# A decoder layer's last expert quad: the final weights spread in two parts between transposes and down products, and one way back put ahead of the last product

## What is computed

```python
for g in range(N_GROUPS):
    hid = (silu(einsum('nd,edf->nef', hf, w_gate[g]))
           * einsum('nd,edf->nef', hf, w_up[g]) * combine[:, g, :, None])
    out = out + einsum('nef,efd->nd', hid, w_down[g])
...
x = x + out
return rmsnorm(x, final_norm_g)     # x * rsqrt(mean(x*x) + eps) * g, g of 1024
```

## Time and profile before

| | us |
|---|---|
| median of 3 runs | 439.71 |
| lowest and highest | 438.43, 440.27 |
| the profiled execution, its own time | 438.02 |
| its span, first to last instruction | 436.3 |
| TensorE busy | 395.9 (91%) |
| VectorE, ScalarE busy | 190.4 (44%), 155.0 (36%) |
| mean granted TensorE clock | 0.979 of 2.4 GHz |

### The profile page before, as it was taken

How to read it: one execution, slowest core, us unless ns; L and a number is a source line. 1 busy time by engine, 2 the same in 40 slices (tenths; PEclk the granted TensorE clock), 3 DMA queues, 4 the chain that set the end, 5 groups by cost and what they waited for, 6 DMA issues and landing times.

```text
span 436.3 us, 7016 instructions
## 1 busy us (share of the span) xinstructions
PE 395.9 (91%) x2761; PEld 278.0 (64%) x2761; DVE 190.4 (44%) x358; ACT 155.0 (36%) x299; POOL 36.0 (8%) x80
## 2 busy tenths in 40 slices
PE   7999999999999999999999989899878838758984
PEld 7998897777788888999796634434333303313632
DVE  3675667866667846754655211221212102102123
ACT  6633565576358444485737110100000000001013
POOL 4010122224000000010401200000000000000001
PEclk9999999999999999999999999999999959969999
DMA  7978776767777668897758899999999999999993
GB/s 243 302 223 281 231 263 215 235 206 241 258 241 268 202 232 292 276 332 225 270 218 361 331 424 421 415 420 421 422 422 423 421 421 422 421 421 409 409 380 120
DMA packets 48770, 138.95 MB, mean 318 GB/s; under 512 B 5191, under 2 KB 19559, under 8 KB 39528
## 3 DMA queue, kind: packets, MB, share of 16 engines
q1 hardware_dynamic: 48528, 138.31, 85.0%
q10 hardware_dynamic: 216, 0.28, 0.2%
HBM read 137.54 MB, written 1.05 MB: 318 GB/s over the span
## 4 chain that ended last, share of the span: by engine, by line
PE 75%; DMA 12%; SPq 5%; DVE 3%; ACT 1%; issue 1%; POOL 1%; DVEq 0%; POOLq 0%; ACTq 0%
DMA moe_pair<-in_expert_w_up_dram 12%; PE proj L1407 10%; PE proj L1408 9%; PE proj L1409 9%; PE proj L1833 7%; SPq L428 5%; PE score L1760 4%; PE score L1856 4%; PE attno L1408 2%; PE attno L1409 2%; PE attno L1407 2%; PE attno L1905 2%; PE proj L1787 2%; PE attno L1551 1%; PE probt L1409 1%; PE probt L1408 1%
## 5 line engine op out<-in xcount | busy, mean ns | idle before, releaser
L945 DVE TENSOR_TENSOR w_lo<-w_raw,w_hi 128x1024 fp32r<-128x1024 f32 x64 | 78.3, 1226 | 37.1 <-ACT w_hi L682 36.8
L682 ACT ACTIVATE w_hi<-w_raw 128x1024 fp32r<-128x1024 f32 x64 | 67.9, 1060 | 40.4 <-DMA w_raw<-in_w_in_dram 11.1
L1833 PE MATMUL proj<-moe_pair,moe_x 128*32 128x512 f32 x384 | 47.4, 637 | 19.6 <-DMA moe_pair<-in_expert_w_up_dram 19.6
L1317 DVE TENSOR_TENSOR moe_x<-score,gains_moe 128x256 f32<-128x256 f32 x32 | 13.6, 425 | 93.3 <-PE score L1760 93.1
L887 ACT ACTIVATE hid<-proj 128x256 f32<-128x256 f32 x8 | 3.1, 383 | 136.8 <-PE proj L1833 112.8
L1833 PEld LDWEIGHTS proj<-moe_pair,moe_x 128*32 128x32 f32 x384 | 11.8, 116 | 45.9 <-issue 44.8
L1760 PEld LDWEIGHTS score<-sel,xg 128*128 128x128 f32 x256 | 30.5, 192 | 10.6 <-issue 10.0
L1407 PE MATMUL proj<-hT_hi,w_hi 128*128 128x256 f32 x112 | 32.3, 288 | 0.8 <-DVE w_lo L1024 0.8
L1760 PE MATMUL score<-sel,xg 128*128 128x128 f32 x256 | 32.5, 279 | 0.0
L1409 PE MATMUL proj<-hT_hi,w_lo 128*128 128x256 f32 x112 | 31.7, 283 | 0.0
L1408 PE MATMUL proj<-hT_lo,w_hi 128*128 128x256 f32 x112 | 31.7, 283 | 0.0
(11 more groups left out here) (345 smaller groups left out, 731.9 us busy)
## 6 DMA issues: line engine op xcount, KB each, us to landing
moe_pair<-in_expert_w_gate_dram SPq DMA_DIRECT2D x28, 1024.0 KB, 13.2
moe_pair<-in_expert_w_up_dram SPq DMA_DIRECT2D x28, 1024.0 KB, 15.0
moe_pair<-in_expert_w_down_dram SPq DMA_DIRECT2D x27, 1024.0 KB, 24.9
w_raw<-in_w_in_dram SPq DMA_DIRECT2D x33, 512.0 KB, 4.4
moe_pair<-in_expert_w_down_dram SPq DMA_DIRECT2D x10, 512.0 KB, 6.5
w_raw<-in_xattn_wkv_dram SPq DMA_DIRECT2D x8, 512.0 KB, 4.4
w_raw<-in_mix_out_w_dram SPq DMA_DIRECT2D x8, 512.0 KB, 5.0
moe_pair<-in_expert_w_gate_dram SPq DMA_DIRECT2D x8, 512.0 KB, 20.1
```

The costliest lines, as they stand in the source:

```text
L682: act.activation(w_hi[g % NS][:], w_raw[:, g % NW], ACT.Copy).then_inc(hi_done, 1)
L945: dve.tensor_tensor(w_lo[g % NS][:], w_raw[:, g % NW], w_hi[g % NS][:].bitcast(F32), ALU.subtract)\
L1317: dve.tensor_tensor(moe_x[:, pair], SC[u % 2][:, 0:2 * P].rearrange("p (k s) -> p k s", k=2), gains_moe[:, u // 2, pair].unsqueeze(2) .bro ...
L1833: op = pe.matmul(PJ[0][e * WIN:(e + 1) * WIN, :].rearrange("p (j f) -> p j f", j=2), moe_x[:, k % 4, e * WIN:(e + 1) * WIN], pair[:].rearr ...
```

## The change

The spreads leave `gate_up_by_columns`. The first one (now into `PJ[0]`) stands behind the transposes, before TensorE waits for `hidT`; the second (still into `SC[1]`) stands between the first and the second half of `down_first_columns`. VectorE's two copies to `fin_g` move behind the product that makes `hid` and behind the copy to `selwT`. TensorE's wait for both copies (`fin_g_set`) moves from before the transposes to before the first ways back.

The way back of tile 0 for piece 0 moves ahead of the last product, `down_last_columns(1, 1)`, with its wait for VectorE's copy of that piece. The others follow as: tile 1 piece 0, tile 0 piece 1, tile 1 piece 1. Each now counts its own semaphore step, and ScalarE's wait for the last half is one higher.

```diff
@@ ScalarE
-                    act.wait_ge(back_ps[t][half], more * 2 + 4)
+                    act.wait_ge(back_ps[t][half], more * 2 + 4 + half)
@@ VectorE, behind the copy to selwT
                 if next_experts is None:
+                    for h, bank in enumerate((PJ[0], SC[1])):
+                        dve.wait_ge(fin_g_ps, h + 1)
+                        dve.tensor_copy(fin_g[:, h * 512:(h + 1) * 512], bank[:]).then_inc(fin_g_set, 1)
                     dve.wait_ge(fin_g_set, 2)
@@ TensorE
+            def spread_gains(bank, half):
+
+                pe.matmul(bank[:], ones_row[:], g_row[:, half * 512:(half + 1) * 512], start=True, stop=True)\
+                    .then_inc(fin_g_ps, 1)
...
             def back_last_columns(t, i):
 
+                pe.wait_ge(y1_sb_set, i + 1)
...
+                    .then_inc(back_ps[t][1], 1)
...
                 gate_up_by_columns(LAST_QUAD, n, ends_in, LAST_UP)
+                transposes(n, hid_halves)
+                pe.wait_ge(fin_in, 16)
+                pe.wait_ge(ones_row_set, 1)
+                spread_gains(PJ[0], 0)
+                pe.wait_ge(hidT_sb, n + 1)
+                down_first_columns(0)
+                pe.wait_ge(selT_sb, n + 1)
+                spread_gains(SC[1], 1)
+                down_first_columns(1).then_inc(y0_ps, 1)
                 pe.wait_ge(fin_g_set, 2)
-                transposes(n, hid_halves)
-                pe.wait_ge(hidT_sb, n + 1)
-                down_first_columns().then_inc(y0_ps, 1)
-                pe.wait_ge(selT_sb, n + 1)
                 pe.wait_ge(y_act, n + 1)
...
                 down_last_columns(0, 1).then_inc(y1_ps, 1)
+                back_last_columns(0, 0)
                 pe.wait_ge(last_cols_in, 16)
                 down_last_columns(1, 1).then_inc(y1_ps, 1)
+                back_last_columns(1, 0)
                 for t in range(TT):
-                    for i in range(2):
-                        pe.wait_ge(y1_sb_set, i + 1)
-                        op = back_last_columns(t, i)
-                    op.then_inc(back_ps[t][1], 1)
+                    back_last_columns(t, 1)
```

More of the change, by code:

```diff
@@ L1328, in expert_quad @@
                 dve.wait_ge(slots_moved, n + 1)
[L1329 to L1332, removed]
                 dve.wait_ge(silu_done, n + 1)
@@ L1797, in gate_up_by_columns @@
                     for j in range(2):
[L1798 to L1804, removed]
                         for pair in range(2):
@@ L1877, in down_whole, with down_first_columns @@
                 return op
[L1879 to L1886, removed]
-                return op
+            def down_first_columns(kt):
+                c = GU_CHUNKS + kt
+                pe.wait_ge(ends_in[c], LAST_LANDED)
+                w = slots[slot_of_chunk(LAST_QUAD * MOE_CHUNKS + c)]
+                for e in range(QE):
+                    op = down_product(0, kt, e, w[:, e * 512:(e + 1) * 512])
+                return op
+            def spread_gains(bank, half):
+                pe.matmul(bank[:], ones_row[:], g_row[:, half * 512:(half + 1) * 512], start=True, stop=True)\
+                    .then_inc(fin_g_ps, 1)
             def down_last_columns(i, kt):
@@ L1898, in back_last_columns @@
             def back_last_columns(t, i):
-                return pe.matmul(ACC[t][1][:, i * CW:(i + 1) * CW], selwT[:, t * P:(t + 1) * P],
-                                 y1_last[:, i * CW:(i + 1) * CW], start=False, stop=True, skip_group_check=True)
+                pe.wait_ge(y1_sb_set, i + 1)
+                pe.matmul(ACC[t][1][:, i * CW:(i + 1) * CW], selwT[:, t * P:(t + 1) * P],
+                          y1_last[:, i * CW:(i + 1) * CW], start=False, stop=True, skip_group_check=True)\
+                    .then_inc(back_ps[t][1], 1)
             def back_to_tokens(t, half):
```

## The result

The changed kernel takes 442.96 us (median of 4 runs, 441.23 to 443.06) against 439.89 us for the kernel before (4 runs). The ratio is 1.0078, with a 95% interval of 1.0062 to 1.0094: 3.4 us slower by the ratio and 3.1 us between the medians, where 1.0 us was forecast. The profiled execution took 441.23 us, the shortest of the four, with a span of 439.5. That is 3.2 us more than the span before, so the two traces side by side show a loss of the full size.

What follows compares the result with a forecast made beforehand. TensorE's chain from 416 us, with load landings close behind, was taken as the bound. Terms of −0.19, +1.31 and −0.07 gave +1.05, taken as +1.0 on 439.7: 440.7 us, range 438.9 to 442.0.

Steps and rivals of the forecast that it cites:

- three signs that I had named: Signs of a wrong forecast: last product before 428.2, a load holding it, or a clock row not 1.00 up to 431.
- The bounds: End of the kernel from 416 us: TensorE's chain with load landings close behind; landings stay, up products start at 416.7.
- Part 1: Spreads moved from in front of the up products: −1.91 + 0.38 + 0.34 + 1.00, a gain of 0.19 us.
- the price of a change of shape: First instruction behind a wait or change of shape takes 0.1 longer, so each moved spread was taken as 1.0 us.
- The bound that I named, 0: Lower limit of the gain from moving the spreads: 0 if each spread costs 1.1 us.
- The wait for `fin_g_set`: Wait for VectorE's copies, now before the first ways back: priced at nothing, with 0.9 us in hand.
- Part 2: Way back ahead of the last product: that product 1.31 us behind its place in the queue, VectorE's scaling 1.05 later.
- The wait of 0.73: Before the moved way back, TensorE waits 0.73 us for VectorE's copy of the third small product's result.
- The way back itself: The moved way back, two instructions ahead of the last product: 0.54 us plus 0.04 for the change of shape.
- The clock: TensorE's granted clock over the tail: expected at 1.00 up to 431, adding nothing to the sum.
- the rival that names it: Clock halves in the new pause before 428.7, the work left takes twice as long: +3.3 us, 443.0; chance 0.04.
- the new pause: TensorE's new wait of 0.7 us behind the third small product, taken as short against the earlier 7.8 us.

Runs made afterwards that it cites:

- the two versions with the old tail: Changed kernel with the second spread in the wait for ScalarE's copy and last ways back in old order: 0.9990 with one-row spreads, 0.9986 with 128-row spreads.
- the part alone: Kernel before with only the new order of the last ways back, spreads left in front of the up products: ratio 1.0022.
- full_rows: Changed kernel with both spreads over all 128 rows (127 rows of zeros behind the weights' row), same order and waits: ratio 1.0031, median 440.71 us.
- filled_wait: Changed kernel plus two unused 128-row products in TensorE's wait before the first ways back, spreads still one row: ratio 1.0053.
- part1_only: Changed kernel with the ways back of the last columns in their old order, spreads still one row: ratio 1.0030, median 441.06 us.

## Why the prediction was wrong, step by step

Two of the three signs that I had named did not come: the last product started at 430.83, not before 428.2, and no load held it. The third came, a clock row that is not 1.00 up to 431.

**The bounds: right.** The up products began at 416.76 for 416.7, and the landings stayed. The last landing proved to be the floor, as the two versions with the old tail show.

**Part 1: the sign was wrong by a small size.** The transposes (419.25 for 419.20) came as worked out. The term that was mis-sized is the price of a change of shape. I took 1.0 for a spread and 0.86 for a block of down products. Measured from start to start: the first spread 1.06, the block 0.99, the second spread 1.05, and the first one started at 419.62 for 419.45. Against the 0.86 in which either would stream, a spread between two blocks lost 0.19 and the block between two spreads 0.13; I had counted 0.14 and nothing. Together this made the second block start at 422.72 for 422.31, and a gain of 0.19 a loss of 0.22. The bound that I named, 0, did not hold it. The wait for `fin_g_set`, which I had put at nothing, did cost nothing: VectorE's second copy was over at 423.52, and the ways back waited for ScalarE.

**Part 2: right.** The last product was to come 1.31 us behind its place and came 1.36 behind it; the part alone measured 1.0 us (0.4 to 1.6), and in its profile the same 2.68 us stand from the first small product to the last. The wait of 0.73 for VectorE's copy was there to the hundredth (0.55 of it shown as idle behind the modelled end of the product). The way back itself took 0.63 from start to start for my 0.54 + 0.04, which is the 0.05 by which 1.31 was short. VectorE's scaling ended the chain, although ScalarE's second square came 0.59 behind the first and not 0.70.

**The clock: the step that failed.** The sum puts it at nothing, and the rival that names it got a chance of 0.04; it decides the result. In the two traces the fall makes the first ways back 1.67 us longer, out of 3.25. With the clock at 1.00 in `full_rows` the change costs 1.0031, 1.4 us, close to the forecast's 1.0. Of the rest up to 1.0078 or 1.0082, some 2 us, 0.2 is the first spread's shorter time over 128 rows, and the fall is what the runs show for the remainder. The rival named the right price range (443.0) by accident, since its place and its cause were wrong. I took the clock to answer to pauses, looked at the pauses of the tail, found them short against the 7.8 us in the earlier trace rows, and put the danger into the new pause behind the third small product. The fall came earlier, at 424.7, and in `filled_wait` it came in a stretch without any pause. I had counted a spread as work, 0.95 us of a busy engine, while the profile shows its operands as 1x512: one row of 128. The products before and after it are over 128 rows, or four pieces side by side. The Trainium skill (TensorE: Matmul & The Clock Gate, what is actually happening) has the gate follow how busy TensorE was. By the busy column of the profile the trace does not agree, as 2.90 of 2.90 us busy went ahead of a fall. It would agree if a one-row product were not taken as busy; the 128-row versions fit that reading but do not prove it.

**Why the kernel before does not show it.** It has the same two spreads, one behind the other in 1.91 us, with dense expert products on both sides and no waits near. In the changed kernel they stand among transposes, waits and each other. That this is the reason is argued, not shown; shown is that with the same spreads in the old place none of 86 runs had a mean clock below 0.968, that with both in the places of the change 14 of 27 did, that with the second in the wait for ScalarE none of 21 did, and that it takes both to be one row wide.

**Left open.** What decides whether an execution has the fall was not found. The version with part 1 over 128 rows, and the two with the second spread in the wait and the old order of the last ways back are 0.10 to 0.14% faster than before, with intervals that end between 0.9999 and 1.0003. If that is real, where it comes from was not followed up. Also open is why the five runs of `part1_only` with a high mean clock still lie at 438.9 to 441.3 us, around 1 us above the kernel before.

## What to carry to other kernels

Before moving a product into a gap, look at its operand's rows in the trace, not only at its time: a product of one row keeps TensorE busy in the profile and here cost its clock in some executions, and the price then fell on the products behind it (1.67 us). Widening it with rows of zeros took no longer and kept the clock. And a wait placed ahead of the last product of a chain cost its whole round trip (0.73 us here, and 0.63 for the product moved), unless a load is later than that; look for the landing time before calling it a gap.

## What the runs showed that was not expected

The clock fell in a stretch in which TensorE was busy without a break (2.90 of 2.90 us), and stayed up in one in which it was idle for nearly a third (1.95 of 2.80 us). A product of 512 columns that streams in 0.86 us took 1.05 between two groups of 32-wide pieces, and a group of such pieces 0.99 between two wide products. Between such groups a product took the same time over one row of weights as over 128 (1.05 us from start to start in both); behind the transposes it took 1.06 over one row and 0.95 over 128. The landings ran evenly: in all fourteen traces the last columns came 11.5 to 11.9 us behind their issue, wherever that lay between 415.9 and 417.8.
